# Value products ahead of three turns, turned copies behind the softplus sums, and the first border chunk in halves

## The chip, the cores and the metric

One core of a Trainium2 chip runs the whole program in one launch. The metric is device time in microseconds (us); the kernel before took 2446.07 us, the median of 3 runs (2444.88 to 2446.53). Engines: PE is TensorE (matrix products), PEld its weight loads, DVE is VectorE, ACT is ScalarE, POOL is GpSimd, SP is SyncE, which issues the weight transfers.

## What is computed

Eight residual sections over 512 tokens of width 1024: a gated feed-forward block (ffn0), an attention mixer (attn), two feed-forward blocks (ffn1, ffn2), an mLSTM mixer, a feed-forward block (ffn3), a pooling and state-space mixer (even) and a convolution mixer (odd). Each section normalises x, computes a branch and adds the normalised branch to x. The attention mixer has 8 stick-breaking heads and 8 dilated heads:

```python
# stick-breaking, per head
z = q @ k.T * scale
log_keep = where(causal, log_sigmoid(-z), 0)
later = cumsum(log_keep, reverse=True) - log_keep
out = exp(where(causal, log_sigmoid(z) + later, -inf)) @ v
# dilated, per head: scores with a bias by distance, softmax, times v
p = softmax(q @ k.T / sqrt(dh) + bias)
out = p @ v
# border of two sections
x = x + rms_norm(branch, g_post)
xn = rms_norm(x, g_pre_of_the_next_section)
```

## The kernel before

Every matrix product is done in three passes over a high and a low part of weights and activations (xh, xl; wh, wl): SyncE loads 512 KB weight blocks into a ring of four, ScalarE makes the high part (L385), GpSimd the low part (L393), TensorE multiplies (L2112 to L2114). All five engines run their own instruction streams in order; the order in each is written out by hand, and semaphores (`wait_ge`, `then_inc`) tie them together.

**Attention** runs in units u = 0 to 9. Unit u computes one stick-breaking head u and its dilated partner. In each unit TensorE (`attention_tensor`, L737 to L761) does in this order: the logits and the scores of unit u (L647, L664, and the causal mask, L652); turns 1 and 2 of unit u-1 (`turn`, L717: the softmax rows of the dilated head are transposed, query block by query block); the value products of unit u-2 (`both_values`, L729 and L732); turn 3 of unit u-1; the suffix sums of the first three column groups of unit u (`suffix_sums`, L691 and L699); turn 0 of unit u; the suffix sums of the last group. ScalarE (`attention_scalar`) makes the softplus of the logits from absolute value, exponential and logarithm (L769, L771, L777), then the weights from the suffix sums (L783). VectorE (`attention_vector`) adds the bias to the scores (L844), takes row maxima (L851), completes the softplus (`spare_sum`, L836, three parts), normalises rows (L861) and copies turned tiles 1 and 2 to SBUF (`take_turned`, L869); ScalarE copies turned tiles 3 and 0 (L798). GpSimd adds up three small sums for the suffix sums (L625 to L629).

Two ties matter. Turn 1 and turn 3 write the same PSUM bank, 4, so turn 3 waits for the copy of turn 1 (`a_td`); the bank also holds scores of the next unit, so turn 1 waits for their bias addition (`a_sadd`). And VectorE completes the softplus sums in three parts, of which TensorE needs the first for its first suffix sum:

```python
elif j == 1:
    pe.wait_ge(a_sadd, nth(u + 1, 3) if u + 1 < UNITS else 4 * u + 4)
if j == 3:
    pe.wait_ge(a_td, 2 * u + 1)
# suffix_sums
pe.wait_ge(a_spr, 3 * u + (3, 1, 2)[kb])
```

**A border** ends each of six sections (ffn0, attn, ffn1, ffn2, mlstm, ffn3). TensorE sums squares over channels (`col_sum`, L2060) for the branch's norm, ScalarE takes the root (L2102), VectorE the reciprocal (L2107), TensorE spreads the rate over the partitions (L2067). Then, for the eight 128x512 chunks of x, VectorE scales the branch (`move`, L2641), adds it to x (`add`, L2645), ScalarE makes the high part of the next section's input (`split_x`, L2506) and a second, full copy (L2507) from which GpSimd makes the low part (L424), and TensorE begins the next section chunk by chunk (`first_three`, `three_high`, L2185 and L2186). While VectorE starts, TensorE still does two column sums for the next norm (the 16 L2060 after the spread). Ahead of the border, `branch_out` on ScalarE ends with three operations on the last chunk: square (L2467), scaled copy (L2469), square of the copy (L2471), and then the root (L2102). At the last border (ffn3 to even) ScalarE also sends tables out to a park buffer (L1411) and waits for these transfers ahead of the first high part.

Of the kernel before, what the change touches and what calls it, by code (L numbers as in the profile page):

```python
# [119 lines left out]
def build(nc, x_in, weights, vecs, consts, rel_bias, buckets, w_gates, pool_w, bst, cst, scratch, turn, park, out):  # L120
    ctx = ExitStack()
    with ctx:
# [109 lines left out]
        root_ready = sem("root_ready")  # L232
        rate_ready = sem("rate_ready")
        spread = sem("spread")
        line_out = sem("line_out")
        mask_loaded = sem("mask_loaded")
        mask_turned = sem("mask_turned")
        gates_loaded = sem("gates_loaded")
# [210 lines left out]
        def strip_scalar(act):  # L449
            act.wait_ge(prep_pe, 1)  # L450
            act.activation(lines[0:HEADS, :].rearrange("p (a n) -> p a n", a=2),
                           banks[0:HEADS, 4:6, 0:320], ACT.Copy).then_inc(prep_act, 1)
            act.wait_ge(prep_act, 1)
            act.dma_start(bass.AP(tensor=scratch.tensor, offset=scratch.offset, ap=[[STRIP_W, HEADS], [1, STRIP_W]]),
                          lines[0:HEADS, :]).then_inc(line_out, 16)

        def strip_copies(act):
            act.wait_ge(line_out, 16)
            row = HEADS * STRIP_W
            act.dma_start(bass.AP(tensor=scratch.tensor, offset=scratch.offset + row, ap=[[row, P], [1, row]]),  # L460
                          bass.AP(tensor=scratch.tensor, offset=scratch.offset, ap=[[0, P], [1, row]])
                          ).then_inc(strip_out, 16)
# [179 lines left out]
        def attention_tensor(pe, value_tiles, out_chunks):  # L642
# [95 lines left out]
            for u in range(UNITS + 2):  # L738
                if u < UNITS:
                    logits_and_scores(u)  # L740
                if u == 0:
                    value_tiles(1)
                if u == UNITS:
                    both_values(u - 2)
                if 1 <= u <= UNITS:
                    for j in (1, 2):
                        turn(u - 1, j)
                if u == UNITS + 1:
                    pe.wait_ge(a_w, 2 * UNITS)
                    out_chunks((0, 1, 2))  # L750
                if u >= 2 and u != UNITS:
                    both_values(u - 2)
                if 1 <= u <= UNITS:
                    turn(u - 1, 3)
                if u < UNITS:
                    suffix_sums(u, (1, 2, 3))
                    if u == 0:
                        pe.wait_ge(tiles_freed, FREE0 + TILE["attn.v"] + 8)
                        score(0, 3)
                    turn(u, 0)  # L760
                    suffix_sums(u, (0,))  # L761
# [70 lines left out]
        def attention_vector(dve):  # L832
            def spare_sum(u, part):
                dve.wait_ge(a_ln, 3 * u + Z_THIRDS.index(part) + 1)
                buf = third(sp_, part)
                dve.scalar_tensor_tensor(buf, z_third(part), 0.0, buf, ALU.max, ALU.add).then_inc(a_spr, 1)  # L836

            def add_bias(u, j):
                qb = ROWS[j]
                n = P * (qb + 1)  # L840
                dve.wait_ge(a_s, nth(u, max(j, 1)))
                if u > 1:
                    dve.wait_ge(a_t, 4 * u + j - 7)
                dve.tensor_tensor(ssb[u % 2][qb][:, 0:n], score_place(j), strip[:, other(u), T - n:T],  # L844
                                  ALU.add).then_inc(a_sadd, 1)

            def row_maximum(u, j):
                qb = ROWS[j]
                n = P * (qb + 1)
                dve.wait_ge(a_sadd, nth(u, j))  # L850
                dve.tensor_reduce(small[:, NMX + qb:NMX + qb + 1], ssb[u % 2][qb][:, 0:n], AX.X, ALU.max,  # L851
                                  negate=True).then_inc(a_mx, 1)

            def normalise(u, j):
                qb = ROWS[j]
                n = P * (qb + 1)
                dve.wait_ge(a_exp, 4 * u + j + 1)
                dve.reciprocal(small[:, RL + qb:RL + qb + 1], small[:, LSUM + qb:LSUM + qb + 1]).then_inc(a_rl, 1)
                dve.wait_ge(a_rl, 4 * u + j + 1)
                rows = ssb[u % 2][qb][:, 0:n]  # L860
                dve.tensor_scalar(rows, rows, small[:, RL + qb:RL + qb + 1], None,  # L861
                                  ALU.mult).then_inc(a_p, 1)

            def take_turned(u, j):
                dve.wait_ge(a_t, 4 * u + j + 1)
                if u > 1:
                    dve.wait_ge(a_odl, u - 1)
                qb = ROWS[j]
                dve.tensor_copy(pT[u % 2][:, 0:qb + 1, P * qb:P * (qb + 1)],  # L869
                                banks[:, TURN_BANK[j], 0:P * (qb + 1)].rearrange("p (a n) -> p a n", n=P)  # L870
                                ).then_inc(a_td, 1)

            def low_of(done, bank, pair, n):
                dve.wait_ge(a_oh, n)
                c = pair + 4 * (bank - 6)
                dve.tensor_tensor(xl[:, c, :], banks[:, bank, :], xh_f[:, c, :], ALU.subtract).then_inc(done, 1)

            dve.wait_ge(strip_in, 16)
            for u in range(UNITS + 2):
                if u < UNITS:  # L880
                    add_bias(u, 0)
                    add_bias(u, 1)
                if 1 <= u <= UNITS:
                    normalise(u - 1, 3)
                if u < UNITS:
                    row_maximum(u, 0)
                    row_maximum(u, 1)
                    if u:
                        add_bias(u, 3)
                    if u:  # L890
                        row_maximum(u, 3)
                    add_bias(u, 2)
                if 1 <= u <= UNITS:
                    take_turned(u - 1, 1)
                if u < UNITS:
                    row_maximum(u, 2)
                    for part in Z_THIRDS:
                        spare_sum(u, part)
                if 1 <= u <= UNITS:
                    take_turned(u - 1, 2)  # L900
                if u < UNITS:
                    normalise(u, 0)
                    if u == 0:
                        add_bias(u, 3)
                        row_maximum(u, 3)
                    normalise(u, 1)
                if u >= 3 and u % 2:
                    low_of(a_oev, 6, (u - 3) // 2, u - 2)
                    low_of(a_oev2, 7, (u - 3) // 2, u - 1)
                if u < UNITS:  # L910
                    normalise(u, 2)
# [1536 lines left out]
        def _(act):  # L2448
            def branch_out(name):
# [8 lines left out]
                for m in range(KD):  # L2458
# [8 lines left out]
                    act.activation(buf[:, S0[m % 2], :], lin[m % 4], ACT.Square).then_inc(branch_sq, 1)  # L2467
                    if last:
                        act.activation(hf[:, m, :], lin[m % 4], ACT.Copy, scale=g).then_inc(branch_sq, 1)  # L2469
                        act.wait_ge(branch_sq, 24 * p + 3 * m + 2)  # L2470
                        act.activation(buf[:, SG[m % 2], :], hf[:, m, :], ACT.Square).then_inc(branch_sq, 1)  # L2471
                        act.wait_ge(cols_summed, EVENT[name + ".post"] + 1)
                        root_scalar(act, EVENT[name + ".post"], sums[0])
                    else:
                        act.activation(buf[:, SG[m % 2], :], lin[m % 4], ACT.Square, scale=g).then_inc(branch_sq, 1)
                        act.activation(hf[:, m, :], lin[m % 4], ACT.Copy, scale=g).then_inc(branch_sq, 1)  # L2476
# [21 lines left out]
            def split_x(name):  # L2498

                event = EVENT[name + ".pre"]  # L2500
                for c in range(KD):
                    if c == KD - 1:
                        act.wait_ge(cols_summed, event + 1)
                    act.wait_ge(x_ready, 8 * (event // 2 - 1) + c + 1)
                    g = g_of(name + ".pre", c)
                    act.activation(xh[:, c, :], x[:, c, :], ACT.Copy, scale=g).then_inc(x_high, 1)  # L2506
                    act.activation(hf[:, c, :], x[:, c, :], ACT.Copy, scale=g).then_inc(hi_ready, 1)  # L2507
                    if c == 4:
                        high_part(act, name + {"attn": ".qk", "mlstm": ".qk", "even": ".in"}.get(name, ".gu"), 0)
                        act.wait_ge(fresh_ready, event // 2 + 1)  # L2510
                        root_scalar(act, event, x_sq)
# [74 lines left out]
        def _(dve):  # L2586
# [10 lines left out]
            def post(name):  # L2597
# [49 lines left out]
                def next_stat():  # L2647
# [5 lines left out]
                    link(dve, dve.tensor_tensor(x_sq, sums[2], x_sq, ALU.add))  # L2653
                    dve.tensor_scalar(x_sq, x_sq, 0.0, None, ALU.max).then_inc(fresh_ready, 1)

                dve.wait_ge(spread, event + 1)
                move(0)
                add(0)
                move(1)
                add(1)  # L2660
                move(2)
# [303 lines left out]
```

## Time and profile before

| | us |
|---|---|
| median of 3 runs | 2446.07 |
| the profiled execution | 2444.48 |
| its span (first to last instruction) | 2441.6 |
| TensorE busy | 2410.4 |
| GpSimd busy | 1307.7 |
| VectorE busy | 1035.4 |
| ScalarE busy | 982.8 |

Mean granted TensorE clock: 0.999 of full speed. TensorE is busy 99% of the span, but a busy TensorE row is an average over stages: in most of the program it multiplies without a break, and the attention loop and the borders are where it can wait for others. Times in the timeline are counted from the first instruction. An instruction on ScalarE or VectorE can begin a little before the one ahead of it has ended.

### The profile page before, as it was taken

The numbers are of one execution on the slowest core, as the hardware profiler recorded it, in microseconds if no ns is written. First come the engines' busy times: TensorE is split into PE (matmuls) and PEld (weight loads), VectorE is DVE, ScalarE is ACT, GpSimd is POOL, SyncE is SP. The second block draws the span as 40 slices with busy tenths as digits, with TensorE's granted clock in tenths as the row PEclk, the third lists the DMA queues.
The fourth block names the chain that finished last, engine by engine and source line by source line (L and its number), as shares of the span: only waits on it lengthen the run. The fifth ranks groups of instructions, "written<-read, shape, count | busy, mean of one in ns | idle before, by whom it ended". The sixth has DMA issues, their size and how long they took to land.

```text
span 2441.6 us, 30816 instructions
## 1 busy us (share of the span) xinstructions
PE 2410.4 (99%) x11236; PEld 1965.4 (80%) x11236; DVE 1035.4 (42%) x1549; ACT 982.8 (40%) x1349; POOL 1307.7 (54%) x724
## 2 busy tenths in 40 slices
PE   9999999999999999999999999999999999999998
PEld 7888888866888888888888888778888888877676
DVE  4222313046522211322241473455222594837985
ACT  5333334266633333433333433545333435345454
POOL 4555545421565554565554544547555556467774
PEclk9999999999999999999999999999999999999999
DMA  4333433310333333233333232213322456334652
GB/s 155 94 97 101 147 103 121 95 44 1 98 101 95 94 103 103 92 97 94 94 104 103 95 95 87 61 41 106 96 94 94 129 160 210 115 103 127 156 138 78
DMA packets 80139, 251.65 MB, mean 103 GB/s; under 512 B 9876, under 2 KB 14484, under 8 KB 79933
## 3 DMA queue, kind: packets, MB, share of 16 engines
q1 hardware_dynamic: 72528, 235.55, 31.3%
q10 hardware_dynamic: 6684, 11.90, 1.5%
q0 software_dynamic: 848, 3.15, 0.4%
q8 instruction: 50, 0.82, 0.1%
q14 instruction: 29, 0.23, 0.0%
HBM read 237.54 MB, written 15.25 MB: 104 GB/s over the span
## 4 chain that ended last, share of the span: by engine, by line
PE 85%; issue 5%; POOL 4%; DVE 3%; DMA 1%; ACT 1%; SPq 0%; DVEq 0%; POOLq 0%; ACTq 0%
PE banks L2112 23%; PE banks L2114 23%; PE banks L2113 23%; POOL wl_sb L393 3%; PE banks L2185 1%; PE banks L2186 1%; PE banks L2191 1%; PE banks L2060 1%; PE banks L729 1%; PE banks L973 1%; PE banks L982 1%; PE banks L691 1%; POOL xl_sb L424 1%; PE banks L2368 1%; PE banks L2370 1%
## 5 line engine op out<-in xcount | busy, mean ns | idle before, releaser
L393 POOL TENSOR_TENSOR wl_sb<-raw_sb,wh_sb 128x1024 fp32r<-128x1024 f32 x401 | 969.6, 2419 | 820.7 <-ACT wh_sb L385 818.2
L2112 PE MATMUL banks<-xh_sb,wh_sb 128*128 128x512 f32 x2043 | 798.9, 391 | 3.3 <-POOL wl_sb L393 2.8
L2113 PE MATMUL banks<-xh_sb,wl_sb 128*128 128x512 f32 x2043 | 795.2, 389 | 0.0
L2114 PE MATMUL banks<-xl_sb,wh_sb 128*128 128x512 f32 x2043 | 795.1, 389 | 0.0
L385 ACT ACTIVATE wh_sb<-raw_sb 128x1024 fp32r<-128x1024 f32 x401 | 424.7, 1059 | 743.9 <-DMA raw_sb<-weights 734.0
L2112 PEld LDWEIGHTS banks<-xh_sb,wh_sb 128*128 128x128 f32 x2043 | 383.6, 188 | 92.1 <-POOL wl_sb L393 6.6
L2114 PEld LDWEIGHTS banks<-xl_sb,wh_sb 128*128 128x128 f32 x2043 | 383.5, 188 | 80.2
L2113 PEld LDWEIGHTS banks<-xh_sb,wl_sb 128*128 128x128 f32 x2043 | 383.6, 188 | 78.9 <-issue 0.2
L2112 PE MATMUL banks<-hh_sb,wh_sb 128*128 128x512 f32 x704 | 274.0, 389 | 0.5 <-POOL wl_sb L393 0.5
L2114 PE MATMUL banks<-hl_sb,wh_sb 128*128 128x512 f32 x704 | 273.9, 389 | 0.0
L2113 PE MATMUL banks<-hh_sb,wl_sb 128*128 128x512 f32 x704 | 273.9, 389 | 0.0
L2690 DVE TENSOR_TENSOR hf_sb<-banks,rstd_sb 128x512 f32<-128x512 f32 x88 | 60.8, 691 | 379.5 <-PE banks L2114 376.9
L2736 POOL TENSOR_TENSOR hl_sb<-hf_sb,hh_sb 128x512 f32 (+1 forms) x88 | 114.0, 1295 | 134.4 <-ACT hh_sb L2522 134.4
L2687 DVE TENSOR_TENSOR hf_sb<-banks,rstd_sb 128x512 f32<-128x512 f32 x88 | 60.9, 692 | 253.0 <-PE banks L2114 251.8
L2522 ACT ACTIVATE hh_sb<-hf_sb 128x512 f32 (+1 forms) x88 | 55.6, 632 | 265.3 <-DVE hf_sb L2693 265.3
L2112 PEld LDWEIGHTS banks<-hh_sb,wh_sb 128*128 128x128 f32 x704 | 132.2, 188 | 28.1 <-POOL wl_sb L393 0.9
L2113 PEld LDWEIGHTS banks<-hh_sb,wl_sb 128*128 128x128 f32 x704 | 132.2, 188 | 27.6
L2114 PEld LDWEIGHTS banks<-hl_sb,wh_sb 128*128 128x128 f32 x704 | 132.2, 188 | 27.4
L2693 DVE TENSOR_TENSOR hf_sb<-hf_sb 128x512 f32<-128x512 f32 x88 | 136.4, 1550 | 8.8 <-ACT hf_sb L2518 6.1
L2610 DVE SCALAR_TENSOR_TENSOR xs_sb<-banks,vecs_sb,x_sb 128x512 f32<-128x512 f32 x28 | 21.0, 750 | 254.8 <-ACT hf_sb L2476 254.8
L424 POOL TENSOR_TENSOR xl_sb<-hf_sb,xh_sb 128x512 fp32r<-128x512 f32 x72 | 96.3, 1357 | 50.6 <-ACT hf_sb L2507 37.9
L2518 ACT ACTIVATE hf_sb<-hf_sb 128x512 f32<-128x512 f32 x88 | 55.7, 633 | 118.6 <-DVE hf_sb L2687 118.6
(434 smaller groups left out, 2657.6 us busy)
## 6 DMA issues: line engine op xcount, KB each, us to landing
raw_sb<-weights SPq DMA_DIRECT2D x404, 512.0 KB, 3.5
park<-xs_sb ACTq DMA_DIRECT2D x12, 512.0 KB, 3.7
mix_sb<-scratch SPq DMA_DIRECT2D x16, 258.0 KB, 5.5
hf_sb<-scratch SPq DMA_DIRECT2D x16, 258.0 KB, 5.3
mix_sb<-park SPq DMA_DIRECT2D x4, 1024.0 KB, 7.3
scratch<-scratch ACTq DMA_DIRECT2D x1, 2560.0 KB, 12.0
scratch<-mix_sb SPq DMA_DIRECT2D x8, 259.5 KB, 2.9
x_sb<-x_in SPq DMA_DIRECT2D x8, 256.0 KB, 7.4
```

The costliest lines, as they stand in the source:

```text
L385: act.activation(wh[:, slot, :], raw[:, slot, :], ACT.Copy).then_inc(w_hi, 1)
L393: pool.tensor_tensor(wl[:, slot, :], raw[:, slot, :], wh_f[:, slot, :], ALU.subtract).then_inc(w_split, 1)
L424: pool.tensor_tensor(xl[:, c, :], hf[:, c, :], xh_f[:, c, :], ALU.subtract).then_inc(xn_ready, 1)
L2112: pe.matmul(dst, wh[:, q, cols], in_hi, start=first, stop=False)
L2113: pe.matmul(dst, wl[:, q, cols], in_hi, start=False, stop=False)
L2114: return pe.matmul(dst, wh[:, q, cols], in_lo, start=False, stop=last)
L2518: act.activation(sg[:, s, :], sg[:, s, :], ACT.Silu).then_inc(gate_act, 1)
L2522: act.activation(at(hh, 2 * i + s), ht[:, s, :], ACT.Copy).then_inc(h_hi, 1)
L2687: dve.tensor_tensor(sg[:, s, :], lin[2 * s], rstd[:, :], ALU.mult).then_inc(gate_scaled, 1)
L2690: dve.tensor_tensor(ht[:, s, :], lin[2 * s + 1], rstd[:, :], ALU.mult).then_inc(tiles_freed, 2)
L2693: dve.tensor_tensor(ht[:, s, :], ht[:, s, :], sg[:, s, :], ALU.mult).then_inc(h_mul, 1)
L2736: pool.tensor_tensor(at(hl, 2 * i + s), ht[:, s, :], at(hh_f, 2 * i + s), ALU.subtract).then_inc(h_lo, 1)
```

## The change

Three edits, and a renaming. In the attention loop TensorE does the value products of unit u-2 ahead of all three turns of unit u-1, and VectorE copies turned tile 1 (with tile 2) behind the three softplus sums instead of ahead of the row maximum. At the borders, chunk 0 of x is scaled, added and split in two halves of 256 columns, crossed on VectorE (scale 0, scale 1, add 0, add 1), with a new semaphore `first_half`. The root of the branch's norm goes ahead of the last square on ScalarE. The semaphore `line_out` is merged into `strip_line`.

```diff
@@ attention_tensor
                 if u == UNITS:
                     both_values(u - 2)
-                if 1 <= u <= UNITS:
-                    for j in (1, 2):
-                        turn(u - 1, j)
                 if u == UNITS + 1:
                     pe.wait_ge(a_w, 2 * UNITS)
                     out_chunks((0, 1, 2))
                 if u >= 2 and u != UNITS:
                     both_values(u - 2)
                 if 1 <= u <= UNITS:
-                    turn(u - 1, 3)
+                    for j in (1, 2, 3):
+                        turn(u - 1, j)
@@ attention_vector
                     add_bias(u, 2)
-                if 1 <= u <= UNITS:
-                    take_turned(u - 1, 1)
-                if u < UNITS:
                     row_maximum(u, 2)
                     for part in Z_THIRDS:
                         spare_sum(u, part)
                 if 1 <= u <= UNITS:
+                    take_turned(u - 1, 1)
                     take_turned(u - 1, 2)
@@ branch_out, last chunk
                         act.activation(hf[:, m, :], lin[m % 4], ACT.Copy, scale=g).then_inc(branch_sq, 1)
+                        act.wait_ge(cols_summed, EVENT[name + ".post"] + 1)
+                        root_scalar(act, EVENT[name + ".post"], sums[0])
                         act.wait_ge(branch_sq, 24 * p + 3 * m + 2)
                         act.activation(buf[:, SG[m % 2], :], hf[:, m, :], ACT.Square).then_inc(branch_sq, 1)
-                        act.wait_ge(cols_summed, EVENT[name + ".post"] + 1)
-                        root_scalar(act, EVENT[name + ".post"], sums[0])
@@ split_x
-                    act.wait_ge(x_ready, 8 * (event // 2 - 1) + c + 1)
                     g = g_of(name + ".pre", c)
-                    act.activation(xh[:, c, :], x[:, c, :], ACT.Copy, scale=g).then_inc(x_high, 1)
+                    if c == 0:
+                        act.wait_ge(first_half, event)
+                        act.activation(xh[:, 0, 0:T // 2], x[:, 0, 0:T // 2], ACT.Copy, scale=g)
+                        act.wait_ge(x_ready, 8 * (event // 2 - 1) + 1)
+                        act.activation(xh[:, 0, T // 2:T], x[:, 0, T // 2:T], ACT.Copy, scale=g).then_inc(x_high, 1)
+                    else:
+                        act.wait_ge(x_ready, 8 * (event // 2 - 1) + c + 1)
+                        act.activation(xh[:, c, :], x[:, c, :], ACT.Copy, scale=g).then_inc(x_high, 1)
@@ post (VectorE)
+                def move_half(h, ready):
+                    cols = slice(h * T // 2, (h + 1) * T // 2)
+                    dve.tensor_tensor(term(0)[:, cols], hf[:, 0, cols], banks[:, 7, cols], ALU.mult).then_inc(ready, 1)
+                def add_half(h, ready):
+                    cols = slice(h * T // 2, (h + 1) * T // 2)
+                    dve.tensor_tensor(x[:, 0, cols], x[:, 0, cols], term(0)[:, cols], ALU.add).then_inc(ready, 1)
                 dve.wait_ge(spread, event + 1)
-                move(0)
-                add(0)
+                move_half(0, first_half)
+                move_half(1, scaled)
+                dve.wait_ge(first_half, 2 * p + 1)
+                add_half(0, first_half)
+                dve.wait_ge(scaled, moved_ + 1)
+                add_half(1, x_ready)
```

## Rows read from the trace of the kernel before

**Rows 1.** The page, chain that ended last: share of the span by engine

```profile
PE 85%; issue 5%; POOL 4%; DVE 3%; DMA 1%; ACT 1%; SPq 0%; DVEq 0%; POOLq 0%; ACTq 0%
```

**Rows 2.** Stretches, units 1 and 4: length, busy (instructions) PE PEld DVE ACT POOL, clock, DMA

```profile
517.81:528.07 10.26, 8.49 (x50) 5.86 (x49) 7.67 (x21) 7.74 (x18) 1.29 (x3) 1.00 0.00 0
...
549.22:559.82 10.60, 10.52 (x65) 6.86 (x65) 7.73 (x21) 8.13 (x20) 1.29 (x3) 1.00 0.01 2
```

**Rows 3.** Timeline, unit 4, TensorE: start, length, engine, line, operation, count [idle before]

```profile
552.27 0.33 PE L652 MATMUL banks<-later_r_sb,ident_r_sb 128*128 128x128 f32 x1
552.67 0.84 PE L717 MATMUL banks<-consts_sb,hf_sb 128*128 128x128 f32 x6
553.44 0.64 PE L729 MATMUL banks<-mix_sb 128*64 128x512 f32 x1
...
555.75 0.55 PE L717 MATMUL banks<-consts_sb,hf_sb 128*128 128x128 f32 x3
556.13 1.46 PE L691 MATMUL banks<-mix_sb,consts_sb 128*128 128x384 f32 x6
```

**Rows 4.** Timeline, unit 4, ScalarE

```profile
551.37 0.81 ACT L769 ACTIVATE mix_sb<-banks 128x768 f32<-128x768 f32 x1 [0.53 <-PE banks L652]
```

**Rows 5.** Timeline, unit 4, VectorE

```profile
551.97 0.55 DVE L844 TENSOR_TENSOR hf_sb<-banks,mix_sb 128x384 f32<-128x384 f32 x1
...
555.03 1.62 DVE L836 SCALAR_TENSOR_TENSOR mix_sb<-banks,mix_sb 128x384 f32<-128x384 f32 x3 [0.40 <-ACT mix_sb L777]
556.57 0.68 DVE L869 COPY mix_sb<-banks 128x512 f32<-128x512 f32 x1
```

**Rows 6.** Timeline, unit 1, VectorE and TensorE

```profile
522.05 0.41 DVE L869 COPY mix_sb<-banks 128x256 f32<-128x256 f32 x1
...
522.61 0.52 PE L717 MATMUL banks<-consts_sb,hf_sb 128*128 128x128 f32 x3 [0.67 <-DVE mix_sb L869]
...
523.62 1.62 DVE L836 SCALAR_TENSOR_TENSOR mix_sb<-banks,mix_sb 128x384 f32<-128x384 f32 x3 [0.56 <-ACT mix_sb L777]
524.23 1.56 PE L691 MATMUL banks<-mix_sb,consts_sb 128*128 128x384 f32 x6 [1.10 <-DVE mix_sb L836]
```

**Rows 7.** Timeline, third border (ffn1 to ffn2), all engines

```profile
1006.73 2.90 PE L2060 MATMUL banks<-inv_d_sb,xs_sb 128*128 128x128 f32 x24
...
1008.13 0.63 ACT L2471 ACTIVATE xs_sb<-hf_sb 128x512 f32<-128x512 f32 x1
...
1008.77 0.26 ACT L2102 ACTIVATE cols_sb<-banks,eps_sb 128x4 f32<-128x4 f32 x1
...
1009.47 0.60 PE L2067 MATMUL banks<-consts_sb,cols_sb 128*128 128x128 f32 x4
...
1010.10 0.70 DVE L2641 TENSOR_TENSOR banks<-hf_sb,banks 128x512 f32<-128x512 f32 x1 [0.17 <-PE banks L2067]
1010.83 0.69 DVE L2645 TENSOR_TENSOR x_sb<-x_sb,banks 128x512 f32<-128x512 f32 x1
...
1011.55 0.72 ACT L2506 ACTIVATE xh_sb<-x_sb,vecs_sb 128x512 fp32r<-128x512 f32 x1 [2.52 <-DVE x_sb L2645]
...
1012.18 0.71 ACT L2507 ACTIVATE hf_sb<-x_sb,vecs_sb 128x512 f32<-128x512 f32 x1
...
1012.38 0.47 PE L2185 MATMUL banks<-xh_sb,wh_sb 128*128 128x512 f32 x1 [0.53 <-issue]
```

**Rows 8.** Groups by form, attention, 256 columns: busy us, mean ns | idle before

```profile
L844 DVE TENSOR_TENSOR hf_sb<-banks,mix_sb 128x256 f32<-128x256 f32 x8 | 3.3, 416 | 0.0
...
L790 ACT ACTIVATE hf_sb<-hf_sb,small_sb 128x256 f32<-128x256 f32 x8 | 3.9, 493 | 0.0
```

**Rows 9.** Timeline, last border (ffn3 to even), ScalarE and its transfer queue

```profile
2029.11 0.33 ACTq L1411 DMA_DIRECT2D park<-xs_sb  x1
2032.56 0.72 ACT L2506 ACTIVATE xh_sb<-x_sb,vecs_sb 128x512 fp32r<-128x512 f32 x1 [3.19 <-DMA park<-xs_sb]
```

**Rows 10.** Waits of TensorE: us in total, times, longest

```profile
PE banks L2185 <- issue: 3.8, 6, 1.2
```

More of the change, by code:

```diff
@@ L234, in build @@
         spread = sem("spread")
-        line_out = sem("line_out")
+        first_half = sem("first_half")
         mask_loaded = sem("mask_loaded")
@@ L454, in strip_scalar @@
             act.dma_start(bass.AP(tensor=scratch.tensor, offset=scratch.offset, ap=[[STRIP_W, HEADS], [1, STRIP_W]]),
-                          lines[0:HEADS, :]).then_inc(line_out, 16)
+                          lines[0:HEADS, :]).then_inc(strip_line, 16)
         def strip_copies(act):
-            act.wait_ge(line_out, 16)
+            act.wait_ge(strip_line, 48)
             row = HEADS * STRIP_W
```

## The prediction

> **What bounds the kernel now.** I read the chain that ended last on the profile's page, then the busy time in each stretch of the attention loop, then three stretches of the timeline (unit 4, unit 1, one border), and last the waits of TensorE. The chain is TensorE for 85% of the span [rows 1], so an edit counts only as far as it moves the start of TensorE's next work. The diff touches two places: the attention loop, once per unit, and the six borders between sections.
>
> The attention units start at 517.81 (unit 1), 528.07 (unit 2), and then every 10.6 us. Units 2 to 7 take 10.56 to 10.60 us with TensorE busy 10.5 us of it: TensorE-bound. Unit 1 has no value products yet, takes 10.26 us and leaves TensorE idle for 1.77 us [rows 2]. In unit 4 the reader should see TensorE's order: first two turns at 552.67, value products from 553.44, third turn at 555.75, and directly behind it the suffix sums at 556.13 [rows 3]. The suffix sums need the first of VectorE's three softplus sums, which run from 555.03 to 556.65, a good half microsecond each [rows 5]. So TensorE arrives about half a microsecond after its input is ready; the data are early and TensorE is late. The sums cannot come earlier than they do: ScalarE waits for this unit's logits (0.53 us of idle time ended by TensorE), and starts the softplus at 551.37 [rows 4]; VectorE then has 0.40 us of idle time that ScalarE's logarithm ends [rows 5].
>
> **Value products ahead of the turns** (units 2 to 7; unit 1 has none to move, units 8 and 9 keep their order). The first turn writes the bank whose scores VectorE's bias addition has just read, and it waits for that addition: it ends at 552.52 [rows 5], the turn begins at 552.67. The mask product ahead of it begins at 552.27 and, at some 0.1 us for 128 columns, leaves a hole of about 0.3 us [rows 3]. The products wait only for things of two units ago, so they fill it. Alone, this would save up to 6 x 0.3 = 1.8 us.
>
> **The first turned copy goes behind the softplus sums.** The copy takes 0.41 us [rows 6], and on VectorE the move is free, since VectorE idles before the sums anyway [rows 5]. But look who waits for it. The third turn overwrites the bank that the first turn filled, so on TensorE it waits for this copy, and TensorE is in order: behind the third turn stand the unit's suffix sums, behind these the next unit's logits. Unit 1 shows the link: copy at 522.05 for 0.41 us, turn at 522.61 with 0.67 us of idle time ended by that copy, so turn = end of copy + 0.15 us [rows 6].
>
> Walk of unit 4 with the new order: last softplus sum ends 556.65; the next operation on VectorE starts 0.08 us before that end, as the second copy does now at 556.57 [rows 5]; first copy 556.57 to 556.98; third turn 557.13; suffix sums 0.38 us after the turn's start, as now (555.75 to 556.13) [rows 3], so 557.51. Today 556.13. The unit is longer by 1.38 us. TensorE finishes the products and two turns by about 555.5 and then stands for 1.6 us; the 0.3 us won earlier is inside that stand and worth nothing. From the suffix sums on everything is TensorE's own pace (3.69 us to the next unit's logits at 559.82, the end of the unit [rows 2]), and the next chain on ScalarE begins only behind those logits, so nothing is recovered in the next unit. The second copy and the two normalisations move 0.33 us later and stay ahead of the fourth turn, which follows the suffix sums by 2 us.
>
> Unit 1: sums 523.62 + 1.62 = 525.24, copy 525.16 to 525.57, turn 525.72, suffix sums 526.10 against 524.23 today [rows 6]. These now wait 0.15 us for their second input (3.84 us to the next unit instead of 3.69), which goes: +1.72 us. Attention in all: 6 x 1.38 + 1.72 = **+10.0 us**. Bounds: 1.2 us per unit if the copy's signal costs nothing (+8.9), 1.55 if the copy and turn take 0.15 us longer (+11.2).
>
> **Border halves.** The page names no releaser for the waits, but a table of TensorE's waits shows all six: 3.8 us in total, 1.2 the longest [rows 10], hence about 0.53 for each of the other five. In the border shown [rows 7], the scaled residual starts on VectorE at 1010.10 (0.70 us), the addition at 1010.83 (0.69), ScalarE's high part at 1011.55 (0.72), and TensorE's first product comes at 1012.38 after 0.53 us of idle time. The new order is four halves on VectorE and two on ScalarE. A half is 0.416 us against 0.70 on VectorE and 0.493 against 0.72 on ScalarE [rows 7, 8]; each costs more than half. Today the addition waits 0.03 us for the scaling; with the halves crossed, each starts 0.08 us before the end of the one ahead: 1010.10 + 4 x 0.416 - 3 x 0.08 = 1011.52, as today, with the first half of x at 1011.18. ScalarE: first half 1011.21 to 1011.70, second (starting 0.09 early, as the copy at 1012.18 does now) 1011.61 to 1012.10, against 1012.27. So -0.17 us per border, five times: -0.85. From both sides: if no half overlaps (0.03 us between each) the last half ends at 1012.45, +0.18 per border, +0.9 in all; and no more than the idle 0.53 can go, as TensorE's own column sums fill the time ahead of it: -2.6. I take the middle because back-to-back pairs of different forms overlap by 0.08 in rows 5.
>
> The Trainium skill (Perfetto Trace Analysis, Optimizing Scalar/DVE Operations) speaks against cutting operations up: each instruction pays a fixed access overhead, about 93 ns for ScalarE on SBUF. By it a half on ScalarE would be (0.72 - 0.09)/2 + 0.09 = 0.41 us, an estimate from that page; the row says 0.49, so this case's fixed share is larger than the page's. By the page the two halves on ScalarE would end 0.16 us earlier still, five times 0.8 us, and the total would be 2454.6 instead of 2455.4.
>
> The sixth border (ffn3 to even) is different: ScalarE starts its high part at 2032.56 only after a park transfer has landed [rows 9], when both halves are long there; two halves take 0.49 + 0.40 = 0.89 instead of 0.72, +0.17 us. The transfer is issued at 2029.11 right behind the root; the moved square now stands between them. ScalarE's queue passes it if its wait is already met, which it is (0 us), or else it costs the square's 0.63 us [rows 7]. I take 0.
>
> **Root ahead of the last square.** Nothing: the root starts at 1008.77, right as the square of 0.63 us from 1008.13 ends, and TensorE's spread at 1009.47 follows an unbroken run of 24 column sums of 0.11 us each [rows 7], so an earlier root would not be seen. The square now ends 0.9 us later, at about 1009.65; TensorE wants it behind the spread of four such products, at 1009.91. That cover of 0.26 us hides the delay; where it is gone, the excess is the cost. The two semaphores that are merged wait for the same events: nothing.
>
> **Sum.** 10.0 - 0.85 + 0.17 = +9.3 us. The profiled execution took 2444.48 us around a span of 2441.6, which would become 2453.8; the median of the runs, 2446.07, lies 1.6 us above it: 2455.4.
>
> **Rivals.**
> 1. The copies are done in time (not slower). If the third softplus sum ended by about 5.7 us after the unit's start instead of 7.4, the copy would be over when TensorE has finished products and two turns, and only the 0.3 us per unit would be seen: -1.8 - 0.85 + 0.17 = -2.5, or 2443.6; with the borders at their best (-2.6) 2441.8. For it: VectorE has 0.40 us of idle time before the sums. Against it: that idle time is a wait for ScalarE, whose chain begins with this unit's logits on TensorE.
> 2. The delay is paid once, since the later units find their inputs ready: 1.7 - 0.7, 2447.1. For it: VectorE and ScalarE are busy 7.7 and 8.1 of 10.6 us and have room [rows 2]. Against it: each unit's softplus begins after TensorE's logits, which stand behind the suffix sums.
> 3. The new stands lower TensorE's clock. 1.6 us of idle time in every 12 would have to take the grant from 2.4 to 1.2 GHz for part of each unit; 3 us more per unit gives 2476. Against: unit 1 is idle for 1.77 us at a grant of 1.00 [rows 2]. For: TensorE would stand this long in seven units in a row, not in one.
>
> **How the numbers follow.** Forecast 84%; rival 1 7%, nearly half of it beyond 0.2% (a little more than its best case); rival 2 7%; rival 3 2%. What a measurement of this kernel can tell from no change is about 0.2%, 4.9 us. The forecast's own range is 8.9 - 2.6 + 0.2 = 6.5 to 11.2 + 0.9 + 0.8 = 12.9 us at the ends; that is 2452.6 to 2459.0. I reach down to 2451.5 for a part of rival 2. Slower by over 0.2%: 0.86; within: 0.11; faster: 0.03.
>
> **What would show it.** Units 2 to 7 of about 12.0 us, unit 1 of 12.0; TensorE idle 1.6 us before the third turn, ended by the first copy; suffix sums 8.3 us after the unit's start instead of 6.9. At five borders an idle time of about 0.35 instead of 0.53 us, at the sixth 1.37. Units of 10.3 us would make the prediction wrong at its main step, as would a third turn that starts before the softplus sums are done.

## The result

The kernel after takes 2455.89 us, the median of 6 runs (2454.44 to 2457.02); the kernel before, on the same chip, 2444.74 (6 runs, 2442.49 to 2446.53). The ratio is 1.0046, 95% interval 1.0036 to 1.0057: slower by 11 us, by more than the 0.2% that can be told from no change. The profiled execution took 2454.44 us around a span of 2452.4; before it was 2444.48 around 2441.6. So the spans differ by 10.8 us.

The waits of TensorE in the kernel after (us in total, times, longest) name the new cost in the first line; before, the turns (L717) waited 0.8 us in all for that copy (then L869), and the last line answers to [rows 10]:

```profile
PE banks L717 <- DVE mix_sb L867: 12.6, 8, 3.8
PE banks L1840 <- DMA hf_sb<-scratch: 4.2, 1, 4.2
PE banks L2181 <- issue: 3.4, 6, 1.5
```

Unit 1 starts at 517.06, units 2 to 7 at 530.40 and then every 11.95 to 11.96 us. The stretches of units 1 and 4, columns as in [rows 2]:

```profile
517.06:530.40 13.34, 9.56 (x49) 6.72 (x49) 7.76 (x21) 7.69 (x18) 1.29 (x3) 0.87 0.00 0
554.31:566.26 11.95, 10.52 (x65) 6.86 (x64) 7.82 (x21) 8.13 (x20) 1.28 (x3) 1.00 0.01 1
```

In unit 4 TensorE's busy time is the same 10.52 us as before; the added 1.35 us is idle time. In unit 1 (13.34 us, before 10.26) the busy time itself has grown by 1.07 us, and the granted clock (the column after POOL) is 0.87 instead of 1.00. The timeline of unit 4, TensorE and VectorE, to be read against [rows 3, 5]:

```profile
557.35 0.33 PE L652 MATMUL banks<-later_r_sb,ident_r_sb 128*128 128x128 f32 x1
557.61 0.64 PE L729 MATMUL banks<-mix_sb 128*64 128x512 f32 x1
...
559.91 0.88 PE L717 MATMUL banks<-consts_sb,hf_sb 128*128 128x128 f32 x6
560.12 1.62 DVE L834 SCALAR_TENSOR_TENSOR mix_sb<-banks,mix_sb 128x384 f32<-128x384 f32 x3 [0.61 <-ACT mix_sb L775]
...
561.66 1.01 DVE L867 COPY mix_sb<-banks 128x256 f32<-128x256 f32 x2
...
562.22 0.52 PE L717 MATMUL banks<-consts_sb,hf_sb 128*128 128x128 f32 x3 [1.43 <-DVE mix_sb L867]
...
562.58 1.46 PE L691 MATMUL banks<-mix_sb,consts_sb 128*128 128x384 f32 x6
```

The chain is to be read upwards: suffix sums 0.36 us behind the third turn, the turn 0.15 us behind the end of the first copy, the copy behind three softplus sums. The suffix sums start 8.27 us after the unit; before, it was 6.91. Unit 1, TensorE, against [rows 6]:

```profile
520.34 0.85 PE L717 MATMUL banks<-consts_sb,hf_sb 128*128 128x128 f32 x6
524.97 0.87 PE L717 MATMUL banks<-consts_sb,hf_sb 128*128 128x128 f32 x3 [3.78 <-DVE mix_sb L867]
525.63 2.54 PE L691 MATMUL banks<-mix_sb,consts_sb 128*128 128x384 f32 x6
528.01 0.61 PE L699 MATMUL banks<-mix_sb,negones_sb 128*128 128x128 f32 x4
```

and the same time in stretches (the clock stands ahead of the last two columns):

```profile
521.00:524.00 3.00, 0.19 (x2) 0.00 (x0) 2.20 (x5) 2.97 (x8) 0.03 (x1) 1.00 0.00 0
524.00:525.00 1.00, 0.03 (x1) 0.06 (x2) 1.00 (x3) 0.26 (x2) 1.00 (x3) 0.70 0.00 0
525.00:526.00 1.00, 1.00 (x4) 0.97 (x5) 0.93 (x5) 0.00 (x0) 0.26 (x1) 0.50 0.00 0
...
527.00:528.00 1.00, 1.00 (x5) 0.82 (x4) 0.00 (x0) 0.00 (x0) 0.00 (x0) 0.60 0.00 0
528.00:529.00 1.00, 1.00 (x10) 0.99 (x9) 0.00 (x0) 0.12 (x1) 0.00 (x0) 1.00 0.00 0
```

TensorE stands for 3.78 us in one piece. Within that stand the grant falls from 1.00 to 0.50 (2.4 to 1.2 GHz) and stays there through 526 into 527; the third turn takes 0.87 us instead of 0.52 and the suffix sums 2.54 instead of 1.46.

The third border, against [rows 7]:

```profile
1017.25 2.90 PE L2056 MATMUL banks<-inv_d_sb,xs_sb 128*128 128x128 f32 x24
...
1019.30 0.26 ACT L2098 ACTIVATE cols_sb<-banks,eps_sb 128x4 f32<-128x4 f32 x1 [0.67 <-PE banks L2056]
1019.46 0.62 ACT L2469 ACTIVATE xs_sb<-hf_sb 128x512 f32<-128x512 f32 x1
...
1019.99 0.60 PE L2063 MATMUL banks<-consts_sb,cols_sb 128*128 128x128 f32 x4
...
1020.63 0.76 DVE L2660 TENSOR_TENSOR banks<-hf_sb,banks 128x256 f32<-128x256 f32 x2 [0.27 <-PE banks L2063]
1021.30 0.75 DVE L2664 TENSOR_TENSOR x_sb<-x_sb,banks 128x256 f32<-128x256 f32 x2
1021.75 0.51 ACT L2503 ACTIVATE xh_sb<-x_sb,vecs_sb 128x256 fp32r<-128x256 f32 x1 [1.67 <-DVE x_sb L2664]
...
1022.16 0.49 ACT L2505 ACTIVATE xh_sb<-x_sb,vecs_sb 128x256 fp32r<-128x256 f32 x1
...
1022.75 0.47 PE L2181 MATMUL banks<-xh_sb,wh_sb 128*128 128x512 f32 x1 [0.38 <-issue]
```

The idle time ahead of the first product is 0.38 us at each of five borders, before 0.53. The last border, against [rows 9]:

```profile
2039.34 0.33 ACTq L1407 DMA_DIRECT2D park<-xs_sb  x1
...
2042.89 0.51 ACT L2503 ACTIVATE xh_sb<-x_sb,vecs_sb 128x256 fp32r<-128x256 f32 x1 [2.77 <-DMA park<-xs_sb]
2043.31 0.49 ACT L2505 ACTIVATE xh_sb<-x_sb,vecs_sb 128x256 fp32r<-128x256 f32 x1
...
2043.90 0.47 PE L2181 MATMUL banks<-xh_sb,wh_sb 128*128 128x512 f32 x1 [1.49 <-issue]
```

From the first high part to the first product it is now 1.01 us instead of 0.82; the transfer landed 0.10 us later behind its issue than before. Together: unit 1 +3.08, units 2 to 7 6 x 1.36 = +8.2, five borders -0.75, the sixth +0.29; the sum is +10.8 us, the difference of the spans. Smaller waits differ between the two profiles in both directions and nearly cancel (the one for a transfer, L1840, is 4.2 us where it was 4.7).

### The profile page after: what moved, and what is told of

The parts are those of the page before. It is cut to its first block, busy times and chain, and to the rows that moved or that the text cites. A ratio compares the mean times of both kernels' runs of the same rounds, so it can differ in the third digit from the quotient of the medians.

```text
span 2452.4 us, 30834 instructions
## 1 busy us (share of the span) xinstructions
PE 2412.1 (98%) x11236; PEld 1966.3 (80%) x11236; DVE 1037.3 (42%) x1561; ACT 983.3 (40%) x1355; POOL 1308.4 (53%) x724
## 4 chain that ended last, share of the span: by engine, by line
PE 83%; issue 5%; DVE 4%; POOL 4%; ACT 1%; DMA 1%; SPq 0%; DVEq 0%; POOLq 0%; ACTq 0%
PE banks L2108 23%; PE banks L2109 23%; PE banks L2110 23%; POOL wl_sb L393 3%; DVE banks L2000 2%; PE banks L2181 1%; PE banks L2182 1%; PE banks L2187 1%; PE banks L2056 1%; PE banks L969 1%; PE banks L978 1%; PE banks L691 1%; POOL xl_sb L424 1%; PE banks L2364 1%; PE banks L2365 1%
```

## The experiments

**The two halves of the change alone.** Attention part alone, that is the kernel before with the hunks `attention_tensor` and `attention_vector` of the change:

```diff
-                if 1 <= u <= UNITS:
-                    for j in (1, 2):
-                        turn(u - 1, j)
...
                     both_values(u - 2)
                 if 1 <= u <= UNITS:
-                    turn(u - 1, 3)
+                    for j in (1, 2, 3):
+                        turn(u - 1, j)
...
-                    take_turned(u - 1, 1)
...
                         spare_sum(u, part)
...
+                    take_turned(u - 1, 1)
```

> The attention edits alone; the borders are those of before. Theory A (the third turn waits for the first copy, which stands behind the softplus sums, and the suffix sums wait behind the third turn): units 2 to 7 last 11.95 us and unit 1 13.3 us as in the changed kernel, +11.2 us in all, ratio 1.0046 to before; the idle time at five borders is 0.53 us again. Rival (part of the loss comes from the border edits, which move the wait elsewhere): less than +10 us here.

Measured: 2457.04 us (4 runs), ratio 1.0049 (1.0033 to 1.0064). Units 2 to 7 take 11.96 us with stands of 1.43 us. The attention part is the whole loss. One thing was not expected: unit 1 takes 14.71 us, 1.37 more than in the kernel after, behind the same stand of 3.78 us:

```profile
517.32:532.03 14.71, 10.93 (x49) 7.81 (x48) 7.77 (x21) 8.22 (x19) 1.29 (x3) 0.77 0.00 0
```

The grant is at 0.50 for 6.8 us here (524.07 to 530.90) and for 3.4 in the kernel after. What sets that is open; both lengths also occur in a stretch of code that no edit touches (shown at the end of the next section).

Border part alone, that is the kernel before with the hunks `branch_out`, `split_x` and `post` of the change:

```diff
-                move(0)
-                add(0)
+                move_half(0, first_half)
+                move_half(1, scaled)
...
+                add_half(0, first_half)
...
+                add_half(1, x_ready)
```

> The border halves and the root's new place alone; the attention loop is that of before. From the idle time of TensorE in the changed kernel (0.375 instead of 0.525 us at five borders, 1.49 instead of 1.20 at the sixth): 5 x 0.15 - 0.29 = 0.46 us faster, ratio 0.9998, not to be told from 1. Rival (the borders cost time that the profile of the changed kernel hides behind other variation): slower than before.

Measured: 2444.55 us (11 runs), ratio 0.9997 (0.9988 to 1.0006); five borders at 0.376 us, units as before. Its gain can be seen in the profile and not in the time.

**Which of the two attention edits costs.** VectorE's move alone, in the kernel before:

```diff
-                if 1 <= u <= UNITS:
-                    take_turned(u - 1, 1)
-                if u < UNITS:
                     row_maximum(u, 2)
                     for part in Z_THIRDS:
                         spare_sum(u, part)
                 if 1 <= u <= UNITS:
+                    take_turned(u - 1, 1)
                     take_turned(u - 1, 2)
```

> The kernel before with one part of the change: VectorE copies the first turned tile behind the three softplus sums; TensorE's order stays as it was (two turns, products, third turn). Theory A (the third turn waits for that copy, wherever the products stand): units 2 to 7 of 11.95 us, stands of 1.4 us before the third turn, unit 1 of 13.3 to 14.7 us with a granted clock of 0.5 behind its stand; no border gain, so 2456 to 2457.5 us, ratio 1.0048 to 1.0053, as with the whole attention part. Theory B (it takes the products' move as well, which pushes the first two turns back): units under 11 us, ratio under 1.0015.

Measured: 2456.61 us (4 runs), ratio 1.0048 (1.0032 to 1.0065); units of 11.95 us, unit 1 of 14.72 at a mean clock of 0.77. Unit 4, the third turn:

```profile
563.89 0.52 PE L717 MATMUL banks<-consts_sb,hf_sb 128*128 128x128 f32 x3 [1.31 <-DVE mix_sb L869]
```

The unit is as long as with both edits; the stand is 0.12 us shorter because the hole ahead of the first turn is back. So the copy's move carries the loss, and with the copy that late the products' move neither adds to it nor eases it.

The kernel after, with the copy early again:

```diff
                     row_maximum(u, 2)
+                if 1 <= u <= UNITS:
+                    take_turned(u - 1, 1)
+                if u < UNITS:
                     for part in Z_THIRDS:
                         spare_sum(u, part)
                 if 1 <= u <= UNITS:
-                    take_turned(u - 1, 1)
                     take_turned(u - 1, 2)
```

> The changed kernel with one step undone in part: VectorE copies the first turned tile directly ahead of the three softplus sums, and TensorE keeps the products ahead of the three turns. Theory A: the copy now waits for the turn, which comes 5.6 us after the unit's start, ends at 6.46, the first softplus sum at 6.94 (0.6 us later than ScalarE would allow), suffix sums at 7.0 instead of 8.3, units 2 to 7 of 10.7 us, unit 1 of 10.3 us without the lower clock; 0 us against before (ratio 1.0000). Rival B (the order of TensorE's own work costs, wherever the copy stands): units stay near 12 us, ratio 1.0046.

Measured: 2445.09 us (10 runs), ratio 1.0002 (0.9992 to 1.0011). The loss is gone, yet units 2 to 7 take 10.85 us, 0.26 more than before. Unit 4:

```profile
554.24 0.88 PE L717 MATMUL banks<-consts_sb,hf_sb 128*128 128x128 f32 x6
...
555.28 0.52 PE L717 MATMUL banks<-consts_sb,hf_sb 128*128 128x128 f32 x3 [0.17 <-DVE mix_sb L867]
```

```profile
554.71 0.42 DVE L867 COPY mix_sb<-banks 128x256 f32<-128x256 f32 x1 [0.91 <-PE banks L717]
```

With the products ahead, the first turn comes only 5.6 us after the unit's start (before 3.4), so VectorE now waits 0.91 us for it, and the third turn then waits for the copy. With the copy in this place the products' move is a small loss, not the gain of 0.3 us for which the prediction had priced it. No run has the products moved and the copy where it stood before, ahead of the row maximum, so the loss of that move alone is not measured.

**The third turn out of the way.** If the harm is that the suffix sums stand behind a turn that waits, the turn goes behind them. The kernel after, with:

```diff
-                    for j in (1, 2, 3):
+                    for j in (1, 2):
                         turn(u - 1, j)
                 if u < UNITS:
                     suffix_sums(u, (1, 2, 3))
+                if 1 <= u <= UNITS:
+                    turn(u - 1, 3)
+                if u < UNITS:
```

> The changed kernel with the third turn moved behind the suffix sums of the first three groups on TensorE; the copies stay behind the softplus sums. Theory A: the wait for the copy is still there but is over when TensorE gets to the third turn, so nothing stands behind it: suffix sums 6.4 us after the unit's start (first softplus sum plus 0.05), units 2 to 7 of 10.3 us, unit 1 about 10.6; against before -1.9 in attention and -0.5 at the borders, 2442 us, ratio 0.9991. Rival B (late copies cost by themselves, whatever stands behind the turn, since the fourth turn and the next scores need them): units above 10.6 us, ratio above 1.

Measured: 2445.87 us (11 runs), ratio 1.0001 (0.9992 to 1.0010). The loss goes, which shows the mechanism, but the gain that was expected on top is not there. Units 2 to 7 take 10.59 us, as before. Unit 3, then unit 1, on TensorE:

```profile
546.02 1.56 PE L691 MATMUL banks<-mix_sb,consts_sb 128*128 128x384 f32 x6
...
548.09 0.65 PE L717 MATMUL banks<-consts_sb,hf_sb 128*128 128x128 f32 x4
```

```profile
523.49 2.93 PE L691 MATMUL banks<-mix_sb,consts_sb 128*128 128x384 f32 x6 [2.29 <-DVE mix_sb L837]
```

The suffix sums start 6.42 us after the unit's start (before 6.91): they now come right behind the first softplus sum. Of this 0.49 us the third turn takes back 0.33, the first suffix product takes 0.10 longer (1.56 us for the six, as in [rows 6], where it also comes right behind its input), and the suffix products behind the turns start 0.04 later. That is nearly the whole 0.49. So the hole ahead of the first turn is gone, TensorE is busy for 10.59 of 10.59 us, and the unit is no shorter. Unit 1, where TensorE stands for 2.29 us in one piece, takes 11.94 instead of 10.26 us, again at a grant of 0.50.

**The place of the copy as a dose.** The kernel after, with the copy behind the first of the three sums:

```diff
                     for part in Z_THIRDS:
                         spare_sum(u, part)
+                        if part == 1 and u:
+                            take_turned(u - 1, 1)
+                if u == UNITS:
+                    take_turned(u - 1, 1)
                 if 1 <= u <= UNITS:
-                    take_turned(u - 1, 1)
                     take_turned(u - 1, 2)
```

> The kernel after with the first turned copy behind the first of the three softplus sums instead of behind all three. Theory A (the place of the copy on VectorE sets the unit): the copy ends some 1.06 us earlier, so suffix sums about 7.2 us after the start of the unit instead of 8.27 and units 2 to 7 of about 10.9 us instead of 11.95; in unit 1 the stand shrinks from 3.78 to about 2.7 us, which by the 2.29 us stand with a granted clock of 0.5 in the kernel with the third turn behind the suffix sums still lowers the clock: 12.3 to 13.6 us. Total 6 x 0.3 + 2.0 to 3.3 - 0.75 + 0.29 = 3.3 to 4.6 us over the kernel before, ratio 1.0014 to 1.0019. Theory B (the units are long because the products now stand ahead of the turns): units stay at 11.9 us, ratio 1.0045.

Measured: 2447.38 us (10 runs), ratio 1.0013 (1.0003 to 1.0023). Units 2 to 7 take 10.89 us. Unit 4, TensorE, then VectorE:

```profile
558.62 0.52 PE L717 MATMUL banks<-consts_sb,hf_sb 128*128 128x128 f32 x3 [0.37 <-DVE mix_sb L867]
558.97 1.46 PE L691 MATMUL banks<-mix_sb,consts_sb 128*128 128x384 f32 x6
```

```profile
557.58 0.56 DVE L834 SCALAR_TENSOR_TENSOR mix_sb<-banks,mix_sb 128x384 f32<-128x384 f32 x1 [0.61 <-ACT mix_sb L775]
558.06 0.41 DVE L867 COPY mix_sb<-banks 128x256 f32<-128x256 f32 x1
```

The suffix sums start 7.20 us after the unit's start, as worked out. Two sums fewer ahead of the copy take 1.06 us off each unit: the unit follows the copy one for one. Unit 1 has a stand of 2.71 us, a grant of 0.50 behind it, and 12.55 us.

**Unit 1: the clock or the inputs.** In the kernel after, TensorE is kept busy in the stand of unit 1 with products that nobody needs:

```diff
                     for j in (1, 2, 3):
+                        if u == 1 and j == 3:
+                            for i in range(30):
+                                pe.matmul(banks[:, 7, 0:P], negones[:, :], negones[:, :], start=True, stop=True)
                         turn(u - 1, j)
```

> The kernel after with one addition: in unit 1 TensorE runs 30 extra products of 128 columns into bank 7, which nobody reads, ahead of the third turn. In the kernel after TensorE stands there for 3.78 us, and the profile then shows a granted clock of 0.5 for 3.4 us, with the suffix sums taking 2.54 instead of 1.46 us. 30 products at the 0.11 us that such products take in this trace fill 3.3 of the 3.78 us. Theory A (the stand lowers the clock): granted clock 1.00 throughout unit 1, suffix sums 1.46 us, unit 1 at about 11.95 us like the units behind it, instead of 13.34; total 1.35 us under the kernel after, about 2454.5 us, ratio to the kernel before 1.0040. Theory B (unit 1 is long because of what its inputs wait for, the clock record is a by-product): unit 1 stays at 13.3 us, ratio 1.0046.

Measured: 2456.18 us (4 runs), ratio 1.0048 (1.0031 to 1.0065). The fill was sized wrongly: each such product ran as two of 0.112 us, so 60 of them held TensorE for 6.7 us, 2.9 past the copy, and unit 1 took 14.69 us. The grant was 1.00 all through and the suffix sums took 1.46 us; on the unit's length this says nothing. With 15 instead of 30:

> The kernel after with 15 extra products of 128 columns into bank 7, which nobody reads, ahead of the third turn of unit 1. In the run with 30 of them each ran as two passes of 0.112 us, so they filled 6.7 us and pushed the third turn 2.9 us past its input: the grant stayed at 1.00 and the suffix sums took 1.46 us, but the unit's length told nothing. 15 products fill 3.35 of the 3.78 us and end before the copy does. Theory A (the stand lowers the clock, and the low clock lengthens the unit): granted clock 1.00 in unit 1, a remaining stand of 0.4 us, suffix sums 1.46 us, unit 1 of 11.9 to 12.0 us instead of 13.34 (after) or 14.71 (attention part alone); total 1.4 us or more under the kernel after, 2453.4 to 2454.5 us, ratio 1.0040. Theory B (unit 1 is long for another reason, its inputs): unit 1 stays at 13.3 us or more.

Measured: 2453.78 us (5 runs), ratio 1.0034 (1.0020 to 1.0048). Timeline and stretch of unit 1:

```profile
522.75 3.51 PE L754 MATMUL banks<-negones_sb 128*128 128x128 f32 x30
526.70 0.52 PE L717 MATMUL banks<-consts_sb,hf_sb 128*128 128x128 f32 x3 [0.44 <-DVE mix_sb L870]
527.05 1.46 PE L691 MATMUL banks<-mix_sb,consts_sb 128*128 128x384 f32 x6
```

```profile
518.78:530.74 11.96, 11.52 (x80) 9.20 (x79) 7.76 (x21) 7.71 (x18) 1.29 (x3) 1.00 0.00 0
```

The third turn starts 7.92 us after the unit's start, as in the kernel after (7.91): its input comes no earlier. With the grant at 1.00 the unit takes 11.96 instead of 13.34 us. So 1.4 us of unit 1 are the clock's. The whole kernel is 8.6 us above the kernel before that ran beside it, where the kernel after is 11.2 above its own, although it does 3.4 us more of products; the intervals of the two ratios overlap, so it is the profile that decides here.

**The root alone,** in the kernel before:

```diff
+                        act.wait_ge(cols_summed, EVENT[name + ".post"] + 1)
+                        root_scalar(act, EVENT[name + ".post"], sums[0])
                         act.wait_ge(branch_sq, 24 * p + 3 * m + 2)
                         act.activation(buf[:, SG[m % 2], :], hf[:, m, :], ACT.Square).then_inc(branch_sq, 1)
-                        act.wait_ge(cols_summed, EVENT[name + ".post"] + 1)
-                        root_scalar(act, EVENT[name + ".post"], sums[0])
```

> The kernel before with one part of the change: at the borders ScalarE takes the root ahead of the last square. Theory A (worth nothing: TensorE's run of 24 column sums ends behind either order): at the third border the root starts 2.05 us and TensorE's spread 2.74 us after the start of the column sums, as in the kernel before, TensorE's idle time before the first product stays 0.53 us at five borders, span within 1 us of 2441.6. Theory B (the root comes earlier and brings the spread with it): spread 2.5 us or less after the start of the column sums, and a span shorter by up to six times 0.25 us. At the last border the park transfer behind the root would start up to 0.6 us earlier or later if the order matters there.

Measured: a single run of 2443.96 us, span 2442.2. Third border:

```profile
1006.24 2.90 PE L2060 MATMUL banks<-inv_d_sb,xs_sb 128*128 128x128 f32 x24
1008.28 0.26 ACT L2102 ACTIVATE cols_sb<-banks,eps_sb 128x4 f32<-128x4 f32 x1 [0.67 <-PE banks L2060]
...
1008.97 0.60 PE L2067 MATMUL banks<-consts_sb,cols_sb 128*128 128x128 f32 x4
```

Root at 2.04 and spread at 2.73 us behind the start of the column sums; before 2.04 and 2.74 [rows 7]. The root now waits 0.67 us for the column sums, which set its time in either order. The five idle times stay 0.52 to 0.53 us, and at the last border the high part still reaches the product in 0.82 us.

## Why the prediction was right, and where it was off

The forecast was 2455.4 us, slower; 2455.89 was measured. Part of that closeness is luck: the sum was +9.3 us and the spans differ by 10.8, while the kernel before, at 2444.74 in the later runs, lies 1.3 us under the median from which the forecast started.

- **The copy and the third turn** (+1.38 us a unit): right, in mechanism and size. Measured +1.36 a unit, a stand of 1.43 us (forecast 1.6), suffix sums at 8.27 us (forecast 8.3). The runs with the copy behind one sum, with the turn behind the suffix sums and with the copy's move alone show that this wait is the cause.
- **Products ahead, "0.3 us, worthless inside the stand"**: worthless is right, 0.3 is not. The hole was read from the turn's start back to the mask's end; in the runs with the products ahead, the product starts 0.26 us behind the mask where the turn started 0.40 behind it, so 0.14 was to be had. And the step left out what the products push back: the first turn, and the copy behind it. With the copy ahead of the softplus sums again, the units are 0.26 us longer than before. Rival 1 rested on that 0.3 us; neither run in which the third turn no longer waits behind the softplus sums made a unit shorter than before.
- **Unit 1** (+1.72 us): mis-sized; measured +3.08. The third turn came 7.91 us after the unit's start, exactly as walked; everything behind it ran at half the clock for a while. With the clock held at 1.00 by the 15 products, the unit took 11.96 us, +1.70, so the walk was right and the clock's 1.38 us was missing. The failed step is in rival 3: it looked at stands of 1.6 us and held unit 1's 1.77 us at full clock against a loss. It didn't work out that in unit 1, which has no products, the stand would be one piece of 3.8 us (turns done at about 4.1 us, third turn at 7.9). Rival 3 was right for one unit and wrong for the six to which it was put: stands of 1.43 us left the grant at 1.00. Its price, 3 us for a unit, was taken from no row; unit 1 paid 1.38 us in the kernel after and about 2.75 in the two kernels where it took 14.7.
- **Border halves** (-0.17 each): -0.15, the halves overlapping as priced (first ScalarE half to first product 1.00 us). The Trainium skill (Perfetto Trace Analysis, Optimizing Scalar/DVE Operations) says that where ScalarE or VectorE isn't saturated but causes bubbles on other engines, "breaking up instructions may allow work to be completed sooner". The trace agrees at five borders (0.53 to 0.38 us) and not at the sixth, where both halves were ready at once. The prediction had read the same section as speaking against cutting up; there that is said of an engine that is saturated, and ScalarE is busy for 982.8 of 2441.6 us.
- **The sixth border** (+0.17): +0.19 for the halves in the profile of after (0.82 to 1.01 us), and 0.10 for the transfer. In the eleven profiles it was 3.25 to 3.57 us from the park transfer's issue to ScalarE's start, in kernels with halves and without, so the 0.10 is scatter.
- **The root** (0): right.
- **Rival 2** (the delay paid once): refuted by six equal units.

The trace of the kernel before already held a stand that bears on the one in unit 1. In the convolution mixer TensorE waits 4.71 us for a transfer, and the grant falls there too (the wait, then a stretch with columns as in the stretches of unit 1 above):

```profile
PE banks L1844 <- DMA hf_sb<-scratch: 4.7, 1, 4.7
```

```profile
2295.16:2298.57 3.41, 2.84 (x16) 0.59 (x16) 3.31 (x6) 1.72 (x3) 2.44 (x3) 0.50 0.63 245
```

All eleven profiles have this stand, 4.20 to 5.19 us long, in code that no edit touches, and in each the grant goes to 0.50: for 3.41 us in five of them, for 6.83 in six. The run with the turn behind the suffix sums has 3.41 us in unit 1 and 6.83 here. So the 1.37 us between unit 1 of the kernel after and of the attention part alone is not shown to be the work of an edit.

No version was measured faster than the kernel before. The five halved borders alone would be worth 0.75 us, under what a measurement tells, and no order tried makes a unit shorter than TensorE's own 10.5 to 10.6 us.

## What to carry to other kernels

Before a copy is moved on an engine that is idle anyway, look for what it frees: an instruction on an in-order engine that waits for the freed buffer holds up everything queued behind it, and in a loop that costs once per turn. Walk the first, thinner turn of the loop by itself, since a stand that is short in the steady units can be one long piece there and lower TensorE's clock. Look in the trace for a stand of that length before pricing it. An edit that fills a hole in an engine's stream gains only if nothing that was early because of the old order, here the first turn, becomes the next thing waited for.

## What was not expected of the hardware

- Where TensorE had been busy and then stood for 2.29, 2.71 and 3.78 us in one piece, the granted clock went from 1.00 to 0.50 in every profile; with the 4.20 to 5.19 us for the transfer it did so in the stand or up to 1.1 us behind it. Where it stood for 1.43 us, or for 0.67 and 1.10 us with work between, it stayed at 1.00.
- The price of the same 3.78 us stand was not the same: unit 1 took 13.34 us in one kernel and 14.71 and 14.72 us in two others, as the grant stayed at 0.50 for 3.4 or for 6.8 us. What decides between the two is open.
- Useless products in the stand paid for themselves: 3.4 us of them kept the clock and shortened the unit by 1.4 us. The Trainium skill (Perfetto Trace Analysis, Matmul Optimizations) says that the matmul engine scales its power with its utilization, and that matmuls should therefore run back to back in batches; these rows agree as far as the granted clock goes; no run here measures power.
